# The first feed-forward matrix of a decoder layer in seven block products in place of eight

## The reference, cut to what matters

```python
def swiglu(x, w_in, w_out):
    a, b = jnp.split(x @ w_in, 2, axis=-1)     # x: 512 x 1024, w_in: 1024 x 5632
    return (jax.nn.silu(a) * b) @ w_out        # w_out: 2816 x 1024
```

## Time and profile before

| | us |
|---|---|
| median of 3 runs | 891.89 (891.59 to 893.75) |
| profiled execution | 891.73 |
| its span | 890.0 |
| TensorE busy in the span | 879.4 |
| the loop over ten pairs (545.27 to 762.80) | 217.53 |

### The profile page before, as it was taken

The page is one execution under the profiler, slowest core; times in us unless marked ns, Lnnn a source line. Parts: engine busy times, 40 slices in busy tenths (PEclk is TensorE's granted clock), DMA queues, the critical chain, the costliest instruction groups (busy, mean ns, idle before and its releaser), DMA issues.

```text
span 890.0 us, 11559 instructions
## 1 busy us (share of the span) xinstructions
PE 879.4 (99%) x4519; PEld 732.5 (82%) x4519; DVE 420.9 (47%) x780; ACT 292.3 (33%) x544; POOL 53.2 (6%) x85
## 2 busy tenths in 40 slices
PE   8999999999999999999999999999999999999996
PEld 8988898877678888888889788888888888888885
DVE  4344357778533434434767693333333333322344
ACT  4112167238632222222325552222222222111221
POOL 3100000262300000000000010000000000000000
PEclk9999999999999999999999999999999999999999
DMA  8535532330013232326605111222222224323211
GB/s 283 161 95 141 119 96 60 107 95 2 1 49 94 95 95 94 94 94 236 220 18 189 48 49 48 94 94 94 94 94 94 94 94 142 105 102 105 104 81 71
DMA packets 70502, 90.11 MB, mean 101 GB/s; under 512 B 2861, under 2 KB 62071, under 8 KB 70463
## 3 DMA queue, kind: packets, MB, share of 16 engines
...
q0 software_dynamic: 384, 0.43, 0.3%
...
HBM read 87.05 MB, written 2.52 MB: 101 GB/s over the span
## 4 chain that ended last, share of the span: by engine, by line
PE 96%; issue 1%; DVE 1%; DMA 1%; ACT 0%; SPq 0%; DVEq 0%; POOLq 0%; POOL 0%
PE ps L1738 28%; PE ps L1739 28%; PE ps L1740 28%; PE ps L1903 3%; PE ps L1980 2%; PE ps L1940 2%; PE ps L1775 1%; DMA x_nat<-in_x 1%; PE ps L2322 1%; PE ps L2323 1%; PE ps L2324 1%; PE ps L2252 0%; PE ps L1949 0%; PE ps L2255 0%; PE ps L2253 0%
## 5 line engine op out<-in xcount | busy, mean ns | idle before, releaser
L1738 PE MATMUL ps<-xt_hi,w_hi 128*128 128x512 f32 (+1 forms) x688 | 267.6, 389 | 0.2 <-DVE w_lo L1694 0.2
L1739 PE MATMUL ps<-xt_hi,w_lo 128*128 128x512 f32 (+1 forms) x688 | 266.8, 388 | 0.0
L1740 PE MATMUL ps<-xt_lo,w_hi 128*128 128x512 f32 (+1 forms) x688 | 266.8, 388 | 0.0
L1738 PEld LDWEIGHTS ps<-xt_hi,w_hi 128*128 128x128 f32 x688 | 129.2, 188 | 27.4 <-issue 0.6
L1740 PEld LDWEIGHTS ps<-xt_lo,w_hi 128*128 128x128 f32 x688 | 129.2, 188 | 26.4
L1739 PEld LDWEIGHTS ps<-xt_hi,w_lo 128*128 128x128 f32 x688 | 129.2, 188 | 26.3
L895 ACT CAST w_hi<-raw 128x1024 fp32r<-128x1024 f32 (+1 forms) x58 | 60.0, 1037 | 180.4 <-PE ps L1740 172.0
L1178 DVE TENSOR_TENSOR w_lo<-raw,w_hi 128x1024 fp32r<-128x1024 f32 (+1 forms) x58 | 70.1, 1210 | 91.1 <-ACT w_hi L895 90.7
L1694 DVE TENSOR_TENSOR w_lo<-raw,w_hi 128x1024 fp32r<-128x1024 f32 x40 | 48.9, 1222 | 79.1 <-ACT w_hi L1137 79.1
L1487 DVE TENSOR_TENSOR w_lo<-raw,w_hi 128x1024 fp32r<-128x1024 f32 x30 | 36.7, 1223 | 90.1 <-ACT w_hi L1062 90.1
L1137 ACT CAST w_hi<-raw 128x1024 fp32r<-128x1024 f32 x40 | 41.9, 1047 | 78.8 <-PE ps L1740 78.8
...
## 6 DMA issues: line engine op xcount, KB each, us to landing
raw<-in_w_in SPq DMA_DIRECT2D x24, 1024.0 KB, 5.0
raw<-in_w_ffn_in SPq DMA_DIRECT2D x22, 1024.0 KB, 4.9
raw<-in_w_ffn_out SPq DMA_DIRECT2D x11, 1024.0 KB, 4.8
raw<-in_w_mix_out SPq DMA_DIRECT2D x4, 1024.0 KB, 4.8
raw<-in_w_branch_b SPq DMA_DIRECT2D x4, 512.0 KB, 4.0
...
raw<-in_w_xkv SPq DMA_DIRECT2D x2, 1024.0 KB, 5.7
raw<-in_w_in SPq DMA_DIRECT2D x3, 512.0 KB, 4.1
```

Of the source, the lines that this page charges most:

```text
L1738: pe.matmul(dst, a_hi, b_hi, start=start, stop=False)
L1739: pe.matmul(dst, a_lo, b_hi, start=False, stop=False)
L1740: return pe.matmul(dst, a_hi, b_lo, start=False, stop=stop)
```

## The change

The first pair stays as it was. For the other ten pairs, each block n = 0 to 19 of 256 columns (even n: columns of a, odd n: of b) is computed by Winograd's form of Strassen's scheme. x is cut into halves by tokens (LO, HI) and by features (0 to 3, 4 to 7), the weights by features and by columns. Seven products P1 to P7, each of 4 feature tiles x 3 matmuls of 256 tokens, replace the eight that the plain scheme takes. What comes with it:

- once, sums of x: F11, F12 (GpSimd), F21, F22 (VectorE), and of them SUM1, SUM2, SUM4 (VectorE) and SUM3 (GpSimd), each 128x1024 numbers; ScalarE rounds the four SUMs, VectorE takes their rests (`sum_rest`)
- per block, four sums of weight quarters (128x512): t1 and t3 on GpSimd (`weight_sums`), t2 and t4 on VectorE
- per block, seven operands (128x512) rounded by ScalarE (`op_round`) and their rests by VectorE (`op_rest`), into four slots: operand m is rounded when product m-4 has ended
- partial results add up in PSUM; where two outputs share one, ScalarE copies it on: `seed` (bank A to C behind P1), `hold_u2` (behind P6), `hold_u3` (behind P7); VectorE adds them (`add_c22`, `add_c12`)
- SiLU, multiplication, rounding and rest of h by quarters (`silu_left`, `silu_right`, `times_left`, `times_right`) and halves (`silu_second`, `times_second`, `round_first`, `round_second`, `hidden_rest`); the two rounding steps move from VectorE to ScalarE
- VectorE's work on the first pair's results (`first_hidden(0)`, `first_hidden(1)`) stands behind the sums and behind `ffn_block(0)`
- the loads of a block come as two transfers of 512 KB, the loops are unrolled, the first step of the second matrix takes its token tiles in another order, and the loads of the last LayerNorm's factors move behind the first two loads of the second matrix

On TensorE a block's products stand in the order P1(n), P4(n-1), P5(n), P3(n-1), P6(n), P2(n), P7(n). P7(0) waits for SUM3's rest, P3(0) for SUM4's.

The diff, cut to its core:

```diff
+OUT_ORDER = [0, 2, 1, 3]
+N_BLOCK = 2 * (D_FF // P // 2 - 1)
...
+def products_in_order():
+    order = []
+    for n in range(N_BLOCK):
+        order.append(("P1", n))
+        if n:
+            order.append(("P4", n - 1))
+        order.append(("P5", n))
+        if n:
+            order.append(("P3", n - 1))
+        order += [("P6", n), ("P2", n), ("P7", n)]
+    return order + [("P4", N_BLOCK - 1), ("P3", N_BLOCK - 1)]
+PRODUCT = {key: m for m, key in enumerate(products_in_order())}
+LAST = N_BLOCK - 1
+def counted(p):
+    return p if p < PO else p - 2 * N_BLOCK
...
+        def x_sum(j, part):
+            if j == 4:
+                return (xt_hi, xt_lo)[part][:, 0:4, 256:512]
+            return quarter(((s1_hi, s1_lo), (s2_hi, s2_lo), (s3_hi, s3_lo))[j - 1][part])
+        def left_operand(kind, part):
+            x = (xt_hi, xt_lo)[part]
+            if kind == "P1":
+                return x[:, 0:4, 0:256]
+            if kind == "P2":
+                return x[:, 4:8, 0:256]
+            if kind == "P4":
+                return x[:, 4:8, 256:512]
+            return x_sum({"P5": 1, "P6": 2, "P7": 3, "P3": 4}[kind], part)
...
+        def right_operand(kind, n):
+            if kind == "P1":
+                return w_quarter(n, 0, 0)
+            if kind == "P2":
+                return w_quarter(n, 1, 0)
+            if kind == "P3":
+                return w_quarter(n, 1, 1)
+            if kind == "P5":
+                return w_t1[:, :, :]
+            if kind == "P7":
+                return w_quarter(n, 0, 1)
+            return w_t2[:, :, :]
...
+        def op_slot(m, part):
+            w = (w_hi, w_lo)[part][m % 4 // 2]
+            return quarter(w[:, 512 * (m % 2):512 * (m % 2) + 512])
+        def bank_a(n):
+            return ps[:, 4 + 2 * (n % 2), 0:256]
+        def bank_b(n):
+            return ps[:, 5 + 2 * (n % 2), 0:256]
+        def bank_c(n):
+            return ps[:, 2 + n % 2, 256:512]
+        def held(n):
+            return u_a if n % 2 == 0 else ht
...
-            for i in range(FF_PAIR):
-                for q in range(2):
-                    sp.wait_ge(lo_done, i * 4 + (PF + 2 * q - 2))
-                    n0 = i * 256 + q * D_FF
-                    sp.dma_start(raw[q][:, :].rearrange("p (k c) -> p k c", k=KT),
-                                 w_f1[:, :, n0:n0 + 256]).then_inc(raw_in[q], 16)
-            sp.wait_ge(norm_done, 2 * TT)
-            for i, w in enumerate(("ln3_g", "ln3_b")):
-                sp.dma_start(gb[:, i, :], A[w][0:1, :].to_broadcast([P, D])).then_inc(gb_in, 16)
+            for q in range(2):
+                sp.wait_ge(lo_done, PF + 2 * q - 2)
+                sp.dma_start(raw[q][:, :].rearrange("p (k c) -> p k c", k=KT),
+                             w_f1[:, :, q * D_FF:q * D_FF + 256]).then_inc(raw_in[q], 16)
+            for n in range(N_BLOCK):
+                q = n % 2
+                if n < 2:
+                    sp.wait_ge(lo_done, PF + 2 * q + 2)
+                else:
+                    sp.wait_ge(op_lo, PRODUCT["P3", n - 2] + 1)
+                k8 = raw[q][:, :].rearrange("p (k c) -> p k c", k=KT)
+                n0 = (1 + n // 2) * 256 + q * D_FF
+                sp.dma_start(k8[:, 0:4, :], w_f1[:, 0:4, n0:n0 + 256]).then_inc(half_in[q], 16)
+                sp.dma_start(k8[:, 4:8, :], w_f1[:, 4:8, n0:n0 + 256]).then_inc(raw_in[q], 16)
             for n in range(FF_PAIR):
-                sp.wait_ge(lo_done, PO + 2 * n - 2)
+                if n < 2:
+                    sp.wait_ge(op_lo, PRODUCT["P3", LAST - 1 + n] + 1)
+                else:
+                    sp.wait_ge(lo_done, counted(PO + 2 * n - 2))
                 sp.dma_start(raw[n % 2][:, :].rearrange("p (k c) -> p k c", k=2),
                              w_f2[:, 2 * n:2 * n + 2, :]).then_inc(raw_in[n % 2], 16)
+                if n == 1:
+                    sp.wait_ge(prod_done, PRODUCT["P6", LAST] + 1)
+                    for i, w in enumerate(("ln3_g", "ln3_b")):
+                        sp.dma_start(gb[:, i, :], A[w][0:1, :].to_broadcast([P, D])).then_inc(gb_in, 16)
...
+            def left_sums():
+                pool.wait_ge(turn_lo, 4 * TT + 4)
+                pool.tensor_tensor(F11, xt_hi[:, 0:4, LO].bitcast(F32), xt_lo[:, 0:4, LO].bitcast(F32), ALU.add).then_inc(left_sum, 1)
+                pool.tensor_tensor(F12, xt_hi[:, 4:8, LO].bitcast(F32), xt_lo[:, 4:8, LO].bitcast(F32), ALU.add).then_inc(left_sum, 1)
+                pool.wait_ge(left_sum, 1)
+                pool.wait_ge(right_sum, 1)
+                pool.tensor_tensor(SUM3, F11, F21, ALU.subtract).then_inc(sum3_done, 1)
+            def weight_sums(n):
+                pool.wait_ge(half_in[n % 2], 16 * (1 + n // 2))
+                if n:
+                    pool.wait_ge(t2_done, n)
+                    pool.wait_ge(op_lo, PRODUCT["P5", n - 1] + 1)
+                pool.tensor_tensor(w_t1[:, :, :], w_quarter(n, 0, 1), w_quarter(n, 0, 0), ALU.subtract).then_inc(t1_done, 1)
+                pool.wait_ge(raw_in[n % 2], F_IN[n % 2] + 16 * (2 + n // 2))
+                pool.wait_ge(t1_done, n + 1)
+                pool.tensor_tensor(w_quarter(n, 0, 1), w_quarter(n, 1, 1), w_quarter(n, 0, 1), ALU.subtract).then_inc(t3_done, 1)
...
+                if n == 2 * TT:
+                    left_sums()
+                    for b in range(N_BLOCK):
+                        weight_sums(b)
...
+                if p == PO:
+                    act.wait_ge(prod_done, PRODUCT["P5", LAST] + 1)
+                elif PO < p < PO + 3 or PO + FF_T - N_TAIL <= p < PO + FF_T - 2:
+                    act.wait_ge(prod_done, PRODUCT["P7", LAST] + 1 if p == PO + 1 else len(PRODUCT))
...
+            def op_round(kind, n):
+                if n > LAST:
+                    return
+                m = PRODUCT[kind, n]
+                if kind == "P1":
+                    act.wait_ge(half_in[n % 2], 16 * (1 + n // 2))
+                elif kind in ("P2", "P3"):
+                    act.wait_ge(raw_in[n % 2], F_IN[n % 2] + 16 * (2 + n // 2))
+                else:
+                    act.wait_ge({"P5": t1_done, "P6": t2_done, "P7": t3_done, "P4": t4_done}[kind], n + 1)
+                if m >= 4:
+                    act.wait_ge(prod_done, m - 3)
+                else:
+                    act.wait_ge(piece_done, PF + 2)
+                act.copy(op_slot(m, 0), right_operand(kind, n)).then_inc(op_hi, 1)
...
+            def seed(n):
+                act.wait_ge(prod_done, PRODUCT["P1", n] + 1)
+                if n < 2:
+                    act.wait_ge(h_done, n + 1)
+                elif n % 2:
+                    act.wait_ge(m0_done, 2 * (n // 2))
+                act.copy(bank_c(n), bank_a(n)).then_inc(seed_done, 1)
...
+            def hold_u2(n):
+                act.wait_ge(prod_done, PRODUCT["P6", n] + 1)
+                if n % 2:
+                    act.wait_ge(h_done, 2 * (n // 2) + 2)
+                act.copy(held(n)[:, LO], bank_c(n)).then_inc(u2_done, 1)
+            def hold_u3(n):
+                act.wait_ge(prod_done, PRODUCT["P7", n] + 1)
+                act.copy(held(n)[:, HI], bank_c(n)).then_inc(u3_done, 1)
...
+            def ffn_block(n):
+                odd, j = n % 2, n // 2 - 1
+                if n:
+                    hold_u3(n - 1)
+                    op_round("P3", n - 1)
+                seed(n)
+                op_round("P6", n)
+                if odd:
+                    silu_right(n - 1)
+                op_round("P2", n)
+                op_round("P7", n)
+                if not odd and n:
+                    round_first(j)
+                hold_u2(n)
+                op_round("P1", n + 1)
+                if odd:
+                    silu_second(n - 1)
+                else:
+                    silu_left(n)
+                op_round("P4", n)
+                op_round("P5", n + 1)
+                if not odd and n:
+                    round_second(j)
+            first_silu(0)
+            sum_round(1)
+            first_silu(1)
+            sum_round(2)
+            op_round("P1", 0)
+            op_round("P5", 0)
+            sum_round(3)
+            for n in range(N_BLOCK):
+                ffn_block(n)
+                if n == 0:
+                    sum_round(4)
+            split(PO)
+            hold_u3(LAST)
+            op_round("P3", LAST)
+            split(PO + 1)
+            round_first(LAST // 2)
+            round_second(LAST // 2)
+            for n in range(2, FF_T):
...
+            def weight_t2(n):
+                dve.wait_ge(t1_done, n + 1)
+                dve.wait_ge(raw_in[n % 2], F_IN[n % 2] + 16 * (2 + n // 2))
+                if n:
+                    dve.wait_ge(op_lo, PRODUCT["P4", n - 1] + 1)
+                dve.tensor_tensor(w_t2[:, :, :], w_quarter(n, 1, 1), w_t1[:, :, :], ALU.subtract).then_inc(t2_done, 1)
+            def weight_t4(n):
+                dve.wait_ge(op_lo, PRODUCT["P6", n] + 1)
```

(151 more changed lines are left out.)

160 lines of the change are left out of this document (83 added, 77 removed).

## The result

The changed kernel takes **904.86 us** (median of 4 runs, 903.1 to 905.89) against 891.77 for the kernel before on the same chip (4 runs): ratio 1.014, 95% interval 1.0118 to 1.0161. It is slower, as forecast, but by 13.1 us and not by 3, and outside the range of 884 to 903. The profiled execution took 903.10 us, with a span of 901.1.

A forecast was written before the change was run, and what follows sets the result against it. TensorE's matmuls were taken to bound the kernel. Matmuls -15.9, start +6.3, end +1.4, clock +1.3 gave -6.9 us; contention's +5.0, +1.3 and +4.0 made it +3.4: from 891.73 to 895 us, slower, range 884 to 903.

The forecast's parts named there:

- The matmuls: Block products in the loop: 84 matmuls of 256 columns replace 48 of 512, 0.80 us saved per block, -15.9 us.
- The start: Before and in block 0: late sums delay P1(0), P6 and P7(0); +6.3 us from order, +5.0 from contention.
- GpSimd holds VectorE: Start and loop: a GpSimd instruction delays VectorE's two-input ones, 0.9 us per 128x512 meeting, 1.9 per 128x1024.
- the first rival: GpSimd waits for VectorE but doesn't hold it, so the loop stays with TensorE: 885 us, faster; chance 0.25.
- The clock: At the start, TensorE's idles ahead of P7(0) and P1(0) each cost a loss of granted clock, +1.3 us each.
- The end (+1.4): After the loop's last P7, split(PO) stands ahead of hold_u3 on ScalarE; P4 and P3 start late: +1.4 us.
- The loop (+4.0): Steady loop: GpSimd's t3 delays P1's rest and so P4's; a stall of 0.4 us per pair, ten pairs.
- "without contention": Steady loop if GpSimd and VectorE don't disturb each other: the period is TensorE's, 0 us more, least margin 0.3 to 0.6.
- The port-bound loop at 903: Port held for whole instructions, so VectorE with GpSimd sets the loop's period: 1.2 us per pair, 903 us; chance 0.15.
- The rival in which the loop hides its two subtracts: Start held up as forecast, but GpSimd's subtracts cost the loop nothing: 891 us, no change; chance 0.10.

The follow-up runs named there:

- The kernel with all edits: Changed kernel with all block weight sums on VectorE, P4's rounding ahead of silu_left, start reordered (GpSimd makes only F11, held back; third and fourth sums later): 883.26 us.

## Why the prediction was wrong in size

**The matmuls (-15.9): right.** 256-column matmuls start 0.120 apart all through the loop (755.33, 755.45, 755.57). The kernel with all edits has the same 1680 matmuls. Its profiled execution took 882.01 us, 9.7 less than the 891.73 of the kernel before, with 5.5 us of stalls left (3.77, 0.55, 0.39, 0.57 and 0.83, less 0.12 each): 15.2 together.

**The start: near.** Forecast for P1(0), P6 and P7(0): 549.3, 553.4 and 562.0; measured 550.68, 554.99 and 563.66, of which some 0.8 us is a shift from far ahead of the change (it begins in the first microseconds, where TensorE waits 0.8 us for a load of x, and 0.2 in the kernel before). So P7(0) was forecast 0.9 us early. Its idle of 5.56 us ends with sum_rest(3), as named, and went when that was moved. L1832 took 3.30 against about 3.2 forecast, and the turned tile came 1.48 us late (1.60 less 0.12) against 1.36.

**GpSimd holds VectorE: right, and the first rival fell.** The forecast of a meeting was 0.9 us for 128x512 and 1.9 for 128x1024. The largest measured in the changed kernel are 1.14 (a rest of 1.83 at 618.17, less 0.69) and 2.09 (3.31 less 1.22, of GpSimd's 2.38). The Trainium skill ("SBUF — State Buffer", section "Who interferes with whom") calls the pair an exclusive lock that whoever issues first has for the whole instruction; it writes the latter of VectorE's two-port modes, and of two SBUF inputs only that they contend. The trace agrees, for two SBUF inputs too, but for some 0.1 to 0.3 us at the end of each.

**The clock: sum right by luck.** Two losses of 1.3 were forecast. There was one, of 28 x (0.214 - 0.120) = 2.6 us, behind the 5.56 us idle: two products' worth where one was taken. The 3.56 us ahead of P1(0) cost nothing in this execution. The other three executions took 904.70 to 905.89 us at a mean granted clock of 0.989 to 0.992, against 0.994 of the profiled one, so a second loss in them is likely, but not shown.

**The end (+1.4): 0.7.** Only P4 of the last block waited, 0.84 less 0.12.

**The loop (+4.0): the step that failed.** It measured 10.3 us. The prediction wrote that "with hidden_rest and times_second behind it P4's rest ends at 11.45, its due time", and took 0.4 per pair. Its bounds were 0 and 12 us, so the loss fell inside them, but by luck: the 12 were drawn for the port alone, and about half of the loss has another cause. Two things were missed in that walk.
- It followed VectorE's queue; of ScalarE's it named the order (the SiLU, then P4's rounding) but gave the SiLU no wait. But silu_left waits for hidden_rest, and P4's rounding stands behind silu_left. P4's rest can't follow hidden_rest; it comes after silu_left and a rounding more. That alone is 0.54 per pair, 4.8 us in nine gaps, and the steady loop "without contention", put at 0 us more, would have had it too. The kernels with GpSimd idle or cut short show it (0.66 a gap); moving one rounding removes it.
- Contention comes on top of an order that has no margin left: 5.4 to 5.8 us in nine gaps, about 0.6 each where 0.4 was taken. The largest gap, 2.1 us, is in the block whose load lands late, so that both subtracts fall on P4's chain.

From 895.0 to the profiled 903.1 it is 8.1 us: 6.3 the loop, 0.9 and 0.8 the start and its shift, -0.7 the end. The other 0.8 lies in small steps of the loop: behind each of the ten stalls the second matmul starts 0.19 after the first in place of 0.12 (0.7 in all; the forecast had counted this refill in its 0.4), and four more starts are 0.22 to 0.25 apart (0.4).

**The rivals.** The port-bound loop at 903 came near the measured time, but not by its mechanism: VectorE is busy for 84% of the loop, not for all of it (VectorE or GpSimd, for 87%: 180.1 us of the 207.5 from P7(0) to the last P4), and TensorE waits in one place of each pair. Moving one rounding on ScalarE takes nothing off the port, and it took 4.5 of the 10.3 us away. The kernel with all sums on VectorE doesn't decide this rival: a subtract there holds the port for a shorter time than on GpSimd, so it would be faster by this rival too. What that kernel rules out is VectorE's own work as the bound: 24.6 us more of it, and 9.5 us less time. The rival in which the loop hides its two subtracts fell with the nine gaps. The first rival's 885 needed more than a VectorE that nobody holds: with GpSimd's sums of the loop cut short the time is still 896.27, since the order costs its 4.9 us in any case, and the start its own.

**What stays open.** Why the clock falls behind one idle stretch and not another. By the idle stretch ahead of P1(0), and the granted clock over 550 to 556 us: 3.56 us cost nothing in the profiled execution of the changed kernel; 3.56 and 3.57 us gave 0.72 with sum_rest(3) early and with GpSimd's sums cut short, and 0.50 with P4's rounding first; 5.16 us gave 0.72 with GpSimd's first sums held back; 3.08 us gave 0.72 in the three kernels with the sums on VectorE and the old start. In the last kernel 3.77 us ahead of P3(0) gave 1.00. In the loop, 2.11 us cost nothing in the changed kernel, and 2.14 us gave 0.78 over 694 to 700 us with GpSimd's first sums held back. The length alone does not decide it in these runs. The Trainium skill ("TensorE: Matmul & The Clock Gate", section "Why this matters for your kernels") advises against idle gaps between bursts of matmuls, since one can bring the clock to half. The trace agrees in most of these runs, and the last kernel's 3.77 us at 1.00 shows that such a gap does not always cost.
